# Five experts with a fixed place instead of four, and the first group of four as the fourth unit

## The chip, the core and the metric

The kernel runs on one core of a Trainium2 chip. The time is the device time of one execution in microseconds. Three runs of the kernel before gave 1578.7, 1586.66 and 1594.92 us; the median is 1586.66 us.

## What is computed

A decoder trunk of two layers over 272 tokens (16 meta tokens and 256 of x) of width 1024. Each layer is a mixer, a layer norm, a mixture of experts and a layer norm again. The mixers differ and are not touched here. The mixture is the same in both layers:

```
scores = sigmoid(h @ w_router)                       # 64 experts
idx    = the 8 best of the 4 best groups of 8, by scores + bias
w      = 2.5 * scores[idx] / sum(scores[idx])
out    = sum over idx of w * (silu(h @ w_gate[e]) * (h @ w_up[e])) @ w_down[e]
out   += (silu(h @ sh_gate) * (h @ sh_up)) @ sh_down   # one shared expert
```

All weights are float32. An expert has 1024 x 512 gate and up weights (2.097 MB, "gate_up") and 256 x 1024 down weights (1.049 MB), 3.146 MB in all. Every layer reads all 64 experts. The last layer needs only the 256 tokens of x.

## The kernel before

**Units.** The 64 experts are sorted by how many tokens chose them and worked through in 27 units (`WIDTHS`, L67). A unit is a pair (64 rows for each of two experts) or a group of four (32 rows each), so that every unit fills TensorE's 128 rows. The ranks 0 to 43, the fullest experts, go into the pairs, the ranks 44 to 63 into the groups. Before, the units are two pairs, then four times a group and four pairs, then four pairs and a last group: the groups are units 2, 7, 12, 17 and 26. The experts are counted in the order of the units as j = 0 to 63; `rank_at(j)` gives the rank that sits at place j. If an expert had more tokens than its rows, a further round over all pairs would follow (`more_rounds`).

**Fixed experts.** Loading has to start before the routing is known. `FIXED` experts (0 to 3) get the first ranks whatever their tokens are: their sort key has 1e5 added (in `constants`). Their weights are loaded during the mixer before (`load_first_experts`, and by hand in layer 0). The expert at place 4 of the kernel before has rank 44, which is known only when the sort is done.

**Slots.** The weights live in `RING` = 6 slots. Slots 0 to 3 are plain buffers ("upper" in layer 0, "experts" in layer 1). Slot 4 lies in `dense_ring`, half 0, where the shared expert's gate and up weights are until they are used. Slot 5 has its gate_up in "upper" (layer 0) or `x_gate_up` (layer 1) and its down weights in `dense_ring`. `assign_slots` (L86) says which slot each place j gets: the places that are loaded when unit i is done are `LOADS[i]`, and they take the slots which the unit frees, in the order of `FREED_ORDER` where that names the unit.

**One unit on TensorE** (L1795 on): gate_up (L1832), the turn of the next unit's rows (L1811), the turn of the product (L1867), the combination of the unit before into the sum (L1852 in layer 0, L1850 in layer 1), the spread of places for a unit three ahead (L1385, L1386), and down (L1887). Behind unit 2 stand the missing halves of the shared expert (L1348), in unit 3 its down product (L1903).

**The load queue** is SP's, one queue in program order. For unit i (`experts_after`) it waits until gate_up of the unit is done (in the first units for its first half, then the second), issues the gate_up loads into the freed slots, waits until down is done and issues the down loads. Behind unit 2 it waits for the shared halves and issues the gate_up of the expert in the shared slot; its down weights are issued in unit 3, after the shared down product.

**Around the routing** (`norm_and_route`): TensorE turns the scores (L1518), VectorE picks the experts, ScalarE copies the turned rows of the tokens, GpSimd stores them to DRAM (L1495) and gathers the rows of units 0 and 1 (L1420). VectorE sorts the experts (`order`, L1684). SP loads the shared down weights (L1247), waits for the order, and loads the expert at place 4 into slot 5. A barrier ends the block, and the first turn of gathered rows follows (L1811). In layer 0 the region of slot 5's gate_up first holds the router's scaled weights and the scores; they are read for the last time when the scores are turned.

## Time and profile before

| | |
|---|---|
| median of three runs | 1586.66 us |
| the profiled execution | 1585.79 us |
| its span | 1583.9 us |
| TensorE busy | 1451.9 us, 92% |
| VectorE busy | 687.2 us, 43% |
| load queue (q1) | 481.81 MB, 76.9% of 16 engines' span |
| gathers and stores from GpSimd (q0) | 29.05 MB |
| experts of layer 0 | unit 0 from 438.11 us, last group from 898.53 us |
| experts of layer 1 | unit 0 from 1092.14 us, last group from 1551.90 us |

TensorE's busy time includes what the profile models of its ends, so 92% is not 92% of its peak. The page divides the span into 40 slices; in the two expert stages (slices 13 to 23 and 29 to 39) DMA stands at 9 tenths or more with 413 to 425 GB/s, and TensorE mostly at 9, with a 7 where it waits. The shares over the whole span therefore mean little: a change of the experts has to be read from what ends last in those two stages.

### The profile page before, as it was taken

To read this page: it belongs to the slowest core of one execution; us is meant where nothing else is said; L and a number is where in the kernel's file an instruction comes from. 1 tells how busy PE (TensorE), PEld (TensorE's weight loads), DVE (VectorE), ACT (ScalarE), POOL (GpSimd) and SP (SyncE) were. 2 spreads that over 40 slices of the span, in tenths; PEclk is the share of its full clock that TensorE was granted. 3 is DMA by queue.
4 is the path that set the end of the run, shared out by engine and by line. 5 is a ranking of instruction groups with operands and counts; after the bars stand their busy time and mean duration, and the time that the engine had idled before them with its cause. 6 is when DMAs were issued, how large, how long until landed. Compare 5 with 4: busy or idle time off the path is not lost. (4 is left out here: it accounts for less than half of the span.)

```text
span 1583.9 us, 24378 instructions
## 1 busy us (share of the span) xinstructions
PE 1451.9 (92%) x9414; PEld 858.7 (54%) x9414; DVE 687.2 (43%) x1459; ACT 355.3 (22%) x744; POOL 251.2 (16%) x323
## 2 busy tenths in 40 slices
PE   8999888999799999797999979897999999979996
PEld 6788668887546444343454457773443433424442
DVE  3888738731524343333343349034333332323324
ACT  3766455220410111111111130123101111101111
POOL 5789606200100000000000000001000000000000
PEclk9999999899899999898999988998999999989998
DMA  7669362039399999999999973297999999999994
GB/s 275 213 187 241 118 181 80 2 114 394 106 379 422 422 423 425 421 424 423 419 425 421 413 272 149 66 403 288 417 425 421 423 422 424 423 424 421 425 421 190
DMA packets 105968, 512.44 MB, mean 324 GB/s; under 512 B 37220, under 2 KB 42404, under 8 KB 68732
## 3 DMA queue, kind: packets, MB, share of 16 engines
q1 hardware_dynamic: 96028, 481.81, 76.9%
q0 software_dynamic: 9824, 29.05, 4.9%
q8 instruction: 77, 1.26, 0.3%
q14 instruction: 39, 0.32, 0.1%
HBM read 508.92 MB, written 17.10 MB: 332 GB/s over the span
## 5 line engine op out<-in xcount | busy, mean ns | idle before, releaser
L2041 DVE TENSOR_TENSOR e_ac<-e_sl,banks 128x256 f32<-128x256 f32 x54 | 22.7, 421 | 408.1 <-ACT e_sl L1959 408.1
L1832 PE MATMUL banks<-upper,e_xgT 128*64 128x512 f32 (+1 forms) x880 | 195.9, 612 | 2.3 <-DMA upper<-in_moe_gate_up 2.1
L327 PE MATMUL banks<-hT,dense_ring 128*128 128x272 f32 x768 | 185.5, 400 | 5.1 <-DMA dense_ring<-in_w_in 5.1
L1420 POOL DMA_INDIRECT x_xg<-rows_dram,x_idx x54 | 53.8, 996 | 829.7 <-DVE x_idx L1412 823.6
L327 PEld LDWEIGHTS banks<-hT,dense_ring 128*128 128x128 f32 x768 | 147.3, 193 | 39.9 <-DMA dense_ring<-in_w_in 5.4
L1832 PE MATMUL banks<-dense_ring,e_xgT 128*64 128x512 f32 (+1 forms) x288 | 136.2, 629 | 35.7 <-issue 35.7
L1832 PE MATMUL banks<-experts,e_xgT 128*64 128x512 f32 (+1 forms) x720 | 160.8, 609 | 1.3 <-DMA experts<-in_moe_gate_up 1.1
L1959 ACT ACTIVATE e_sl<-banks 128x256 f32<-128x256 f32 x54 | 20.8, 385 | 496.1 <-PE banks L1832 496.1
L1832 PEld LDWEIGHTS banks<-upper,e_xgT 128*64 128x64 f32 (+1 forms) x880 | 64.9, 131 | 90.1 <-issue 90.1
L1852 PE MATMUL banks<-x_sg,route_consts 128*128 128x272 f32 x432 | 104.4, 393 | 0.5 <-DVE acc L2028 0.5
L1850 PE MATMUL banks<-route_consts,x_sg 128*128 128x512 f32 x216 | 97.6, 594 | 0.8 <-DVE acc L2025 0.8
L1832 PEld LDWEIGHTS banks<-dense_ring,e_xgT 128*64 128x64 f32 (+1 forms) x288 | 38.0, 134 | 104.1 <-issue 104.1
L1832 PEld LDWEIGHTS banks<-experts,e_xgT 128*64 128x64 f32 (+1 forms) x720 | 52.9, 132 | 75.9 <-issue 75.9
L2055 DVE COPY route_consts<-banks 128x512 f32<-128x512 f32 x54 | 37.4, 692 | 127.3 <-PE banks L1887 125.3
L2008 DVE TENSOR_TENSOR acc<-acc,banks 128x272 f32<-128x272 f32 x208 | 89.8, 438 | 6.1 <-PE banks L1852 3.0
L1852 PEld LDWEIGHTS banks<-x_sg,route_consts 128*128 128x128 f32 x432 | 79.9, 190 | 17.4 <-issue 1.7
L1887 PE MATMUL banks<-experts,e_aT 128*64 128x512 f32 (+1 forms) x360 | 80.2, 596 | 5.1 <-DVE acc L2013 4.8
L1887 PE MATMUL banks<-dense_ring,e_aT 128*64 128x512 f32 (+1 forms) x304 | 80.0, 595 | 3.6 <-DVE acc L2013 3.0
L1887 PE MATMUL banks<-upper,e_aT 128*64 128x512 f32 (+1 forms) x360 | 80.2, 596 | 1.2 <-DVE acc L2008 1.2
L2013 DVE TENSOR_TENSOR acc<-acc,banks 128x512 f32<-128x512 f32 x100 | 68.8, 688 | 22.3 <-PE banks L1850 19.8
L497 DVE SCALAR_TENSOR_TENSOR upper<-route_consts,conv_w,upper 128x272 f32<-128x272 f32 x64 | 54.1, 845 | 49.4 <-ACT upper L385 38.3
L1832 PE MATMUL banks<-x_gate_up,e_xgT 128*64 128x512 f32 (+1 forms) x160 | 75.0, 624 | 0.0
(453 smaller groups left out, 2130.2 us busy)
## 6 DMA issues: line engine op xcount, KB each, us to landing
upper<-in_moe_gate_up SPq DMA_DIRECT2D x45, 2048.0 KB, 28.0
experts<-in_moe_gate_up SPq DMA_DIRECT2D x36, 2048.0 KB, 27.7
upper<-in_moe_down SPq DMA_DIRECT2D x43, 1024.0 KB, 26.5
experts<-in_moe_down SPq DMA_DIRECT2D x43, 1024.0 KB, 26.5
dense_ring<-in_moe_down SPq DMA_DIRECT2D x38, 1024.0 KB, 25.7
dense_ring<-in_moe_gate_up SPq DMA_DIRECT2D x18, 2048.0 KB, 20.5
dense_ring<-in_w_in SPq DMA_DIRECT2D x47, 512.0 KB, 5.1
upper<-in_moe_gate_up SPq DMA_DIRECT2D x20, 1024.0 KB, 13.3
```

Source lines behind the costliest of these rows:

```text
L327: mm = pe.matmul(ps[g % 4][:, 0:T], slot[:, n % SLOTS_IN, c, :], hT[:, c, :], start=(c == 0), stop=(c == DC - 1))
L497: step.done(dve.scalar_tensor_tensor(out=dst, in0=src[:, j:j + T], scalar=w(j), in1=dst, op0=ALU.mult, op1=ALU.add))
L1420: pool.indirect_dma_start(out=ex["xg"][:, i % 2, :], out_offset=None, in_=mem["rows_dram"], in_offset=bass.IndirectOffsetOnAxis(ap=ex["idx ...
L1832: mm = pe.matmul(gub[e * n:(e + 1) * n, :], xgT[:, i % 2, c, e * n:(e + 1) * n], gate_up_weights(mem, j)[:, c, :], start=(c == 0), stop=(c ...
L1850: pe.matmul(cb[m][:], sg[:, i % 4, tokens], ys[:, columns], start=True, stop=True).then_inc(cmm, 1)
L1852: pe.matmul(cb[m % 4][:, 0:W], ys[:, m * P:(m + 1) * P], sg[:, i % 4, :], start=True, stop=True).then_inc(cmm, 1)
L1887: mm = pe.matmul(yb[e * n:(e + 1) * n, :], aT[:, f, e * n:(e + 1) * n], down_weights(mem, j)[:, f, h * BLOCK:(h + 1) * BLOCK], start=(f == ...
L1959: act.activation(sl[:], gub[:, 0:FF], ACT.Silu).then_inc(sil, 1)
L2008: dve.tensor_tensor(acc[:, m, 0:W], acc[:, m, 0:W], cb[m % 4][:, 0:W], ALU.add).then_inc(addd, 1)
L2013: dve.tensor_tensor(total[:, tile, columns], total[:, tile, columns], cb[m][:], ALU.add).then_inc(addd, 1)
L2041: dve.tensor_tensor(ac[:], sl[:], gub[:, FF:], ALU.mult).then_inc(mul, 1)
L2055: dve.tensor_copy(ys[:, BLOCK:], y1b[:]).then_inc(ye1, 1)
```

## The change

Five experts (0 to 4) have a fixed place. The widths start with three pairs and end with three pairs and a group, so the groups are units 3, 8, 13, 18 and 26. Place 4 is now rank 4, in the third pair; its weights go to slot 5 as before, but SP no longer waits for the order: in layer 0 it waits until the scores are turned, in layer 1 for nothing. `HELD` = 4 keeps what `FIXED` meant for the loads that are issued before the routing. The shared expert still goes with units 2 and 3; the expert that takes its slot is place 11 (before 13). With `FREED_ORDER` down to one entry, the groups of the new kernel sit in slots 1, 2, 3 and 0, and the slots 5 and 4 always hold pairs.

```diff
-FIXED = 4
+FIXED, HELD = 5, 4
...
-WIDTHS = (2, 2) + 4 * (4, 2, 2, 2, 2) + (2, 2, 2, 2, 4)
+WIDTHS = (2, 2, 2) + 4 * (4, 2, 2, 2, 2) + (2, 2, 2, 4)
...
-FREED_ORDER = {2: (0, 5, 1, 2, SHARED_SLOT), 7: (SHARED_SLOT, 5, 1, 2)}
+FREED_ORDER = {2: (0, RING - 1, SHARED_SLOT)}
...
-                for j in range(FIXED):
+                for j in range(HELD):
                     load_down(sp, k, mem, 0, j, j)
...
-def load_expert(sp, k, mem, layer, j):
-
-    load_gate_up(sp, k, mem, layer, expert_at(sp, mem, j), j)
-    load_down(sp, k, mem, layer, expert_at(sp, mem, j), j)
-
-
-def load_first_experts(sp, k, mem, layer, js=range(FIXED)):
+def load_first_experts(sp, k, mem, layer, js=range(HELD)):
...
                 load_shared_down(sp, k, mem, layer)
-                sp.wait_ge(ordered, 1)
-                load_expert(sp, k, mem, layer, FIXED)
+                if layer == 0:
+                    sp.wait_ge(score_turned, 1)
+                load_gate_up(sp, k, mem, layer, HELD, HELD)
+                load_down(sp, k, mem, layer, HELD, HELD)
...
-                dve.tensor_copy(mem["order"][:], sort_ps[0:1, 0:E]).then_inc(ordered, 1)
+                dve.tensor_copy(mem["order"][:], sort_ps[0:1, 0:E])
...
-            "down_low_ready": [sem(f"down_low_{slot}_ready") for slot in range(FIXED)],
+            "down_low_ready": [sem(f"down_low_{slot}_ready") for slot in range(HELD)],
```

The slots of the first places, as the tables give them (place: slot; in brackets the places that are loaded when the unit is done):

```
before                                        after
unit 0  0:0 1:1            (5 6)              unit 0  0:0 1:1            (5 6)
unit 1  2:2 3:3            (7 8)              unit 1  2:2 3:3            (7 8)
unit 2  4:5 5:0 6:1 7:2    (9 10 11 12, 13)   unit 2  4:5 5:0            (9 10, 11)
unit 3  8:3 9:0            (14 15)            unit 3  6:1 7:2 8:3 9:0    (12 13 14 15)
unit 4  10:5 11:1          (16 17)            unit 4  10:5 11:4          (16 17)
```

The number behind a comma is the expert in the shared slot.

SP in the block of layer 0's routing, before. `in_sh_down` are the shared down weights, `order` the sorted experts, `in_moe_gate_up` and `in_moe_down` the weights of the expert at place 4:

```order
L1247 DMA dense_ring<-in_sh_down 128x2x1024
L1257 TENSOR_LOAD order
L1257 ISA x2
L1202 ISA
L1202 DMA upper<-in_moe_gate_up 128x4096
L1257 TENSOR_LOAD order
L1257 ISA x2
L1221 ISA
L1221 DMA dense_ring<-in_moe_down 128x2048
L1477 UNCONDITIONAL_BRANCH
```

The same place after the change:

```order
L1247 DMA dense_ring<-in_sh_down 128x2x1024
L1202 DMA upper<-in_moe_gate_up 128x4096
L1221 DMA dense_ring<-in_moe_down 128x2048
L1471 UNCONDITIONAL_BRANCH
L1743 UNCONDITIONAL_BRANCH
```

The two loads follow the shared down weights with no value read from `order` between them.

TensorE in layer 0 from the end of unit 2's down product to unit 3, before. 32x512 is a product of a group, 64x512 one of a pair; L1348 are the shared expert's halves:

```order
L1887 MATMUL banks<-dense_ring,e_aT 32x512
L1887 MATMUL banks<-upper,e_aT 32x512 x3
L1348 MATMUL banks<-hT,dense_ring 128x272 x16
L1832 MATMUL banks<-upper,e_xgT 64x512 x16
L1811 MATMUL banks<-ident,x_xg 128x128 x8
L1867 MATMUL banks<-ident,e_ac 128x128 x2
L1903 MATMUL banks<-shared_act,dense_ring 128x272 x16
```

And after the change:

```order
L1883 MATMUL banks<-dense_ring,e_aT 64x512
L1883 MATMUL banks<-upper,e_aT 64x512
L1342 MATMUL banks<-hT,dense_ring 128x272 x16
L1828 MATMUL banks<-upper,e_xgT 32x512 x32
L1807 MATMUL banks<-ident,x_xg 128x128 x8
L1863 MATMUL banks<-ident,e_ac 128x128 x2
L1899 MATMUL banks<-shared_act,dense_ring 128x272 x16
```

The pair now stands before the shared halves and the group behind them.

## Rows read from the trace of the kernel before

**Rows 1.** A stretch: busy PE, PEld, DVE, ACT, POOL; clock, DMA share, GB/s.

```profile
740.00:760.00 20.00, 10.24 (x67) 3.04 (x68) 0.00 (x0) 0.25 (x1) 0.00 (x0) 0.66 1.00 419
```

**Rows 2.** Timeline of TensorE, layer 0: start, duration, line, form, idle before and releaser.

```profile
467.72 7.07 PE L1832 MATMUL banks<-upper,e_xgT 128*32 128x512 f32 x64
...
492.52 7.09 PE L1832 MATMUL banks<-upper,e_xgT 128*64 128x512 f32 x32
...
655.60 1.03 PE L1832 MATMUL banks<-dense_ring,e_xgT 128*32 128x512 f32 x1 [8.79 <-issue]
...
749.76 1.03 PE L1832 MATMUL banks<-dense_ring,e_xgT 128*32 128x512 f32 x1 [10.74 <-issue]
...
898.53 3.64 PE L1832 MATMUL banks<-upper,e_xgT 128*32 128x512 f32 x32
...
904.29 3.64 PE L1832 MATMUL banks<-upper,e_xgT 128*32 128x512 f32 x32 [2.12 <-DMA upper<-in_moe_gate_up]
```

**Rows 3.** Timeline of SP's load queue, layer 0.

```profile
430.31 0.38 SPq L1202 DMA_DIRECT2D upper<-in_moe_gate_up  x1
...
441.95 4.27 SPq L1209 DMA_DIRECT2D upper<-in_moe_gate_up  x4
...
471.66 5.21 SPq L1209 DMA_DIRECT2D upper<-in_moe_gate_up  x8
...
493.33 0.33 SPq L1202 DMA_DIRECT2D dense_ring<-in_moe_gate_up  x1
499.80 0.85 SPq L1202 DMA_DIRECT2D upper<-in_moe_gate_up  x2
```

**Rows 4.** Timeline, all engines, of layer 0's routing.

```profile
408.54 0.39 PE L1518 MATMUL banks<-ident,upper 64*128 64x64 f32 x3 [0.86 <-ACT upper L1580]
...
418.80 0.58 POOL L1495 DMA_DIRECT2D rows_dram<-acc  x1 [18.72 <-ACT acc L1591]
```

**Rows 5.** A stretch of 2 us before the first reload of layer 0.

```profile
440.00:442.00 2.00, 2.00 (x13) 0.72 (x10) 0.00 (x0) 0.00 (x0) 0.99 (x1) 1.00 0.02 6
```

**Rows 6.** Timeline of SP's load queue, layer 1.

```profile
1062.96 5.75 SPq L1247 DMA_DIRECT2D dense_ring<-in_sh_down  x1
...
1088.01 0.01 SPq L1221 DMA_DIRECT2D dense_ring<-in_moe_down  x1
1096.64 4.27 SPq L1209 DMA_DIRECT2D experts<-in_moe_gate_up  x4
...
1156.57 0.86 SPq L1202 DMA_DIRECT2D experts<-in_moe_gate_up  x2
```

**Rows 7.** A stretch of 2 us behind the shared expert's loads, layer 1.

```profile
1074.00:1076.00 2.00, 0.00 (x0) 0.00 (x0) 1.76 (x9) 2.00 (x5) 0.00 (x0) 0.50 0.49 199
```

**Rows 8.** Queue's packets, MB, share: 441.95-499.80; 520-840; 430.31-432.31; 442-444; 1096.64-1156.57; 1080-1084.

```profile
q1 hardware_dynamic: 3003, 21.94, 91.6%
...
q1 hardware_dynamic: 11870, 128.83, 95.7%
...
q1 hardware_dynamic: 17, 0.28, 71.2%
...
q1 hardware_dynamic: 6, 0.05, 7.3%
...
q1 hardware_dynamic: 3148, 22.94, 93.1%
...
q0 software_dynamic: 288, 1.05, 66.0%
```

**Rows 9.** Gathers, issue to landing (last number): at 1085, and the median of all.

```profile
x_xg<-rows_dram,x_idx POOLq DMA_INDIRECT x1, 3.8
...
x_xg<-rows_dram,x_idx POOLq DMA_INDIRECT x54, 10.1
```

**Rows 10.** Timeline of TensorE, layer 1.

```profile
1089.56 1.49 PE L1811 MATMUL banks<-ident,x_xg 128*128 128x128 f32 x8 [2.26 <-PEq L174]
...
1556.62 3.64 PE L1832 MATMUL banks<-experts,e_xgT 128*32 128x512 f32 x32 [1.08 <-DMA experts<-in_moe_gate_up]
```

More of the change, by code:

```diff
@@ L1473, in norm_and_route @@
             "keys_ready", "keys_spread", "ranks_ready", "sorted", "count_ready"))
-        warmed, ordered = sem("table_held"), sem("order_ready")
+        warmed = sem("table_held")
         gain = lambda c: ln[:, 4 * layer * DC + c:4 * layer * DC + c + 1]
```

## The prediction

> **What bounds the kernel.** I read the two expert stages first by 20 us stretches, then the order of TensorE's units, then the load queue (SP). In [rows 1] TensorE is busy 10.24 of 20 us while the 16 DMA engines stay at share 1.00 and 419 GB/s: they have no room left. How close the two are is in [rows 2]: a group of four takes TensorE 7.07 us for its gate and up weights, a pair 7.09 us, so a unit costs the same whatever its width, and twice per layer (at the groups in units 12 and 17) TensorE stands for 8.79 and 10.74 us until the last of four experts lands. The last unit, again a group, starts at 898.53 and stops in its middle until 904.29, where the row names a DMA as releaser; in layer 1 it is the same at 1556.62 [rows 10]. So **each expert stage ends by the DMA engines**: by when they begin to run without a break, by the bytes, and by every break in between. From the two stalls I get the price of one expert, gathers beside it included: (749.76 - 655.60) / 12 = 7.85 us.
>
> **Part 1: expert 4 is loaded early.** Before, its load is issued at 430.31, when the order of the experts is known; the first reload (experts 5 and 6 into the slots that unit 0 frees) goes out at 441.95 [rows 3]. Between 440 and 442 the engines move 6 GB/s [rows 5]: the expert is already in, nobody waits for it. After the change it is loaded in idle time before that (layer 0 when the scores are turned, from 408.54 on [rows 4]; layer 1 straight behind the shared expert). The time of the first reload hangs on unit 0's matmuls, and the number of experts loaded after it is 59 in both kernels. So this part **gains nothing** on the path; its cover is the idle time itself.
>
> It has one cost, in layer 1. The shared expert's last load is issued at 1062.96 [rows 6], and the queue has run out between 1074 and 1076, where 199 of some 422 GB/s leave about 0.9 us of work, so at about 1075 [rows 7]. Expert 4 is 3.15 MB, 7.5 us at 422 GB/s: it ends at 1082.4. The rows of the tokens are stored just then, 1.05 MB between 1080 and 1084 on the other queue [rows 8]; alone they need 2.5 us and are over at about 1082.7. At 1080.1 some 1.0 MB of the expert is left; both together, 2.05 MB, need 4.9 us, so the stores end between 1082.7 and 1085.0. The two gathers wait for them: 3.8 us from issue to landing [rows 9], and TensorE turns the gathered rows at 1089.56 [rows 10]. Nearly all of a delay arrives there. Bounds: nothing lost and 0.7 us gained (SP's last load of expert 4, at 1088.01 [rows 6], no longer stands before the barrier that lets TensorE go at 1089.56), or 2.3 us lost. I take 1.2 us, nearer to the loss, because the overlap of the two transfers is sure and the gain is one of several things the barrier may wait for. In layer 0 the stores start at 418.80 [rows 4] and expert 4 is in by 418: nothing.
> The Trainium skill, "DMA: Bandwidth & Descriptors", section "Queues, rings and completion order", says that an engine takes turns between the queues that have work; by it the stores run at half rate while both have bytes and all of the 2.3 us is lost, my upper end. The sum with it would be 1.1 us more.
>
> **Part 2: the pair comes third, the group fourth.** On TensorE the two units only change places, and by [rows 2] every unit starts when it did: unit 2 at 467.72, the halves of the shared expert behind it, unit 3 at 492.52, its gate_up done at 499.6. What changes is how many slots are free. Unit 2 before frees four slots, after it two. SP's queue before: four experts from 471.66 on, the shared slot's expert at 493.33, two more at 499.80 [rows 3]; the engines never pause. After: two experts at 471.66, the shared slot's gate_up at 493.33 (its down weights wait behind, until the shared expert's down product is done), and then nothing until unit 3's gate_up frees four slots at 499.80. So by 499.80 the engines can have moved **at most** experts 5 to 10 and one gate_up: 6 x 3.146 + 2.097 = 20.97 MB. Before, the load queue had moved 21.94 MB by then, and it moves 128.83 MB in 320 us while full, 403 GB/s beside the gathers [rows 8]. The deficit is 0.97 MB = 2.4 us. On top comes the restart: of the load issued at 430.31 only 0.28 MB had moved by 432.31, 0.7 us worth, so it starts 1.3 us after its issue [rows 8]. Issued with a gather under way (441.95), only 0.05 MB had moved by 444, so up to 2.0 us. I take 1.3, since no gather is due at 499.80. **Layer 0: 2.4 + 1.3 = 3.7 us.** Does the earlier hole (experts 9 and 10 landed, 493.33 not yet reached) add to it? No: the gate_up issued there needs 1.3 + 5.2 us and is in at 499.8, so the cap of 20.97 MB is just reached. With a restart of 2.0 us it is missed by 0.7: 5.1 us is the upper end, 2.4 the lower.
> Layer 1, the same way: first reload at 1096.64, unit 3's loads at 1156.57 [rows 6]; 22.94 MB moved in between [rows 8]. Deficit 1.97 MB = 4.9 us, with the restart **6.2 us**, between 4.9 and 7.6.
>
> **Where it goes.** From 500 on the queue is never empty again: four experts at 499.80, as in the groups later. The lost time is not made up, because the engines are the bound at the end of both layers: the waits before 904.29 and 1556.62 mean that a later last expert is later one for one. TensorE's own chain shifts with it (the last group starts 9 units after the group in unit 17 before, 8 units after the one in unit 18 now; (898.53 - 749.76) / 9 = 16.5 us less, against two experts more, 15.7 us), so it stays just behind the engines. All other edits (the removed semaphore, the load that takes a constant instead of a value from the order, the names) cost nothing: DVE and SP have no one behind them there.
>
> **Sum:** 3.7 + 6.2 + 1.2 = 11.1 us on the profiled execution's 1585.79, so 1596.9; the median of the runs shown is 1586.66, 0.9 above. I forecast **1597 us**, 0.7% slower. The ends of the unknowns give 2.4 + 4.9 - 0.7 = 6.6 and 5.1 + 7.6 + 2.3 = 15.0 us.
>
> **Rivals.**
> The forecast (the engines run dry once in each layer, around unit 3): chance 0.62.
> *No hole, or one that is hidden*: the times of SP's issues or the last unit move so that the 2.12 and 1.08 us waits of TensorE swallow it. For it: only 1 to 2 MB are missing. Against: the waits are TensorE's for the engines, not the reverse. 1.2 us remain: 1588. Chance 0.18.
> *Faster*: the load of expert 4 between 430 and 440 did hold up what follows, and with it gone each layer ends one expert, 7.85 us, sooner: 1586.66 - 15.7 = 1571. It decides if the first reload after the change goes out, or lands, several microseconds sooner. Against it stands the empty stretch of [rows 5]. The Trainium skill, "Trainium Kernel Development and Optimization", section "Best Practices", asks to overlap transfers with compute, which is what this load does; by that rule alone the load's move is a gain. Chance 0.06.
> *Slower by more than 1%*: the routing of layer 1 pays. A gather issued while the load queue is full lands after 10.1 us, the median of all 54, against 3.8 us for the one at 1085 [rows 9]. If stores and gather meet expert 4's stream at that price, unit 0 starts 6.3 us late, and the sum is 3.7 + 6.2 + 6.3 = 16.2: 1603. It decides if the stream is still running when the gather is issued. Against it: the stream should be over at 1082.4. Chance 0.13.
> *The order of the experts overflows*: with five fixed experts the first expert in a group of 32 rows could have more than 32 tokens, and a whole extra round of 32 pairs would follow, 64 x 7.85 = 502 us. Counted with the reference on its inputs, that expert has 30 tokens in layer 0 and 29 in layer 1, before and after. Chance 0.01.
>
> **Range and chances.** Runs of the kernel before spread from 1578.7 to 1594.92, so about 1% (16 us) is what tells a change from none. The range reaches from the hidden case less 3 us to the 15.0 us end and the rival behind it, with 3 us for the runs' own spread: 1585 to 1606. Faster by over 1%: the third case, 0.06. Slower by over 1% (1602.5): 0.08 of the fourth case, the fifth, and 0.08 of the forecast's own: 0.17. Between: 0.77.
>
> **What the profile after would show.** The load of expert 4 at about 409 and 1069; the same start of unit 0 in layer 0 and up to 2 us later in layer 1; unit 3 as the first group at 492 with DMA below full share between about 492 and 501, and again around 1148 to 1158; the groups in units 13 and 18 standing for about 11 us each; the last wait still on a DMA, at about 908 and 1568. If the engines are full through 490 to 502, part 2 is wrong; if the stretch is empty and the end has not moved, the claim on the bound is; if the first reload is not at 442, part 1 is.

## The result and the profile after

The kernel after takes 1597.68 us, the median of 11 runs; ten of them lie between 1588.39 and 1600.19 us. The kernel before takes 1587.34 us in 11 runs (1578.7 to 1594.92). The ratio is 1.0046 with a 95% interval of 1.0026 to 1.0065: 7 us slower, between 4 and 10, well under 1%. (One of the 11 runs of the kernel after, 8270.28 us, was disturbed; it is left out of the ratio, and without it the median is 1596.58 us, 9.2 above before.) The forecast was 1597 us.

The profiled execution of the kernel after is its fastest, 1588.39 us, and a reader who compares it with the 1585.79 us of before sees 2.6 us where the medians show 10. So the traces have to be compared by stretches. Unit 0 of layer 0 starts at 430.60 instead of 438.11, by stretches whose work the change does not touch: 5.4 us are the luck of one execution, 2.1 us are TensorE's clock in layer 0's routing (again_after, below). Behind it the stages take longer than they did.

First the order of TensorE's units in layer 0, as in [rows 2]: start, duration, line, form, idle time before and releaser. 128*32 is a product of a group, 128*64 one of a pair.

```profile
460.08 2.34 PE L1828 MATMUL banks<-upper,e_xgT 128*64 128x512 f32 x10
...
484.84 1.50 PE L1828 MATMUL banks<-upper,e_xgT 128*32 128x512 f32 x12
...
667.64 1.94 PE L1828 MATMUL banks<-upper,e_xgT 128*32 128x512 f32 x8 [11.81 <-issue]
...
761.80 2.79 PE L1828 MATMUL banks<-upper,e_xgT 128*32 128x512 f32 x12 [10.98 <-issue]
...
894.65 3.64 PE L1828 MATMUL banks<-upper,e_xgT 128*32 128x512 f32 x32 [0.43 <-issue]
...
899.48 1.06 PE L1828 MATMUL banks<-upper,e_xgT 128*32 128x512 f32 x8 [1.19 <-DMA upper<-in_moe_gate_up]
```

Unit 2 starts 29.5 us behind unit 0, as before (467.72 - 438.11 = 29.6), and unit 3 24.8 us later, as before, now as a group. The groups in units 13 and 18 stand for 11.8 and 11.0 us, and the last wait of the last group is still one for a DMA. From unit 0 to the end of that wait it is 899.48 - 430.60 = 468.88 us against 904.29 - 438.11 = 466.18: **2.7 us more**.

Next the load queue, as in [rows 3]:

```profile
403.59 0.34 SPq L1202 DMA_DIRECT2D upper<-in_moe_gate_up  x1
...
434.46 4.44 SPq L1209 DMA_DIRECT2D upper<-in_moe_gate_up  x4
...
463.89 5.28 SPq L1209 DMA_DIRECT2D upper<-in_moe_gate_up  x4
476.63 0.33 SPq L1221 DMA_DIRECT2D upper<-in_moe_down  x1
477.14 0.33 SPq L1221 DMA_DIRECT2D dense_ring<-in_moe_down  x1
485.66 0.34 SPq L1202 DMA_DIRECT2D dense_ring<-in_moe_gate_up  x1
492.12 1.98 SPq L1202 DMA_DIRECT2D upper<-in_moe_gate_up  x4
```

Expert 4 goes out at 403.59; the first reload comes 3.86 us behind unit 0's start (before: 3.84), so the early load has not brought it forward. Behind unit 2 stand two experts (four halves at 463.89 where [rows 3] show eight), the shared slot's gate_up, and nothing more until 492.12. What the engines did meanwhile stands in two stretches of layer 0 and five of layer 1 (busy PE, PEld, DVE, ACT, POOL; clock, DMA share, GB/s):

```profile
484.00:486.00 2.00, 2.00 (x16) 0.82 (x19) 0.44 (x1) 0.00 (x0) 0.00 (x0) 1.00 0.60 250
...
492.00:494.00 2.00, 2.00 (x14) 1.71 (x14) 1.31 (x3) 1.22 (x3) 0.00 (x0) 1.00 0.82 213
...
1144.00:1146.00 2.00, 2.00 (x11) 1.77 (x10) 0.00 (x0) 0.00 (x0) 0.00 (x0) 1.00 0.26 107
1146.00:1148.00 2.00, 2.00 (x20) 0.74 (x22) 0.42 (x1) 0.00 (x0) 0.00 (x0) 1.00 0.00 0
1148.00:1150.00 2.00, 2.00 (x24) 0.54 (x20) 0.00 (x0) 0.00 (x0) 0.00 (x0) 1.00 0.85 197
...
1154.00:1156.00 2.00, 2.00 (x12) 1.29 (x11) 1.30 (x3) 0.96 (x3) 0.00 (x0) 1.00 0.76 164
1156.00:1158.00 2.00, 2.00 (x6) 0.86 (x5) 0.69 (x1) 0.00 (x0) 0.00 (x0) 1.00 0.86 360
```

Each layer has two breaks: one when the six experts are in (484, 1144), and one when the shared slot's gate_up is all but in too (492, 1154). In layer 1 the engines move nothing at all for over 2 us. TensorE is busy throughout: its row shows nothing of the loss.

In layer 1, as in [rows 10]:

```profile
1086.95 1.09 PE L1807 MATMUL banks<-ident,x_xg 128*128 128x128 f32 x8 [2.18 <-DMA x_xg<-rows_dram,x_idx]
...
1089.13 3.46 PE L1828 MATMUL banks<-experts,e_xgT 128*64 128x512 f32 x10
...
1559.34 1.92 PE L1828 MATMUL banks<-experts,e_xgT 128*32 128x512 f32 x16 [1.18 <-DMA experts<-in_moe_gate_up]
```

Unit 0 to the last wait: 1559.34 - 1089.13 = 470.21 us, before 1556.62 - 1092.14 = 464.48: **5.7 us more**. The routing of layer 1, from its first column sum to unit 0's gate_up, took 31.62 us (from 1060.52) and takes 33.60 us (from 1055.53): **2.0 us more**. The stretch between the layers (156.23 and 156.05 us) and the tail (27.28 and 27.26 us) are as they were. That makes 2.7 + 5.7 + 2.0 = 10.4 us more. Layer 0's routing takes 2.1 us less (37.34 and 39.47 us up to unit 0), which leaves 8.3. The median of the ten undisturbed runs lies 9.2 us above before, the ratio says 7 (4 to 10). That the first sum meets the 10.3 us between the medians of 11 runs is chance.

The stretches of all kernels that were run, each from its one profiled execution, in us; each ratio is to the kernel before in the same set of runs, and again_before is a single run. "Chain" is layer 1's routing up to the issue of the rows' stores (L1491 in the kernel after), "rows" from there to unit 0's gate_up:

| kernel | stage 0 | chain | rows | stage 1 | ratio to before |
|---|---|---|---|---|---|
| before | 466.18 | 18.48 | 13.14 | 464.48 | |
| again_before | 465.99 | 20.18 | 19.65 | 465.57 | |
| after | 468.88 | 18.54 | 15.06 | 470.21 | 1.0046 (1.0026 to 1.0065) |
| again_after | 468.84 | 18.50 | 15.31 | 470.54 | 1.0064 (1.0042 to 1.0086) |
| load_early | 466.49 | 18.48 | 15.84 | 465.01 | 0.9994 (0.9975 to 1.0012) |
| group_fourth_late_load | 469.05 | 18.49 | 12.55 | 470.27 | 1.0059 (1.004 to 1.0078) |
| group_fifth | 475.15 | 21.35 | 12.39 | 476.48 | 1.0112 (1.0081 to 1.0143) |
| shared_short | 467.70 | 20.20 | 13.90 | 464.32 | 0.999 (0.9973 to 1.0007) |
| down_late | 469.01 | 18.49 | 15.35 | 470.62 | 1.0052 (1.003 to 1.0074) |
| shared_behind | 466.34 | 18.50 | 14.71 | 466.21 | 1.0002 (0.9982 to 1.0022) |
| load_at_barrier | 469.45 | 21.41 | 12.42 | 466.71 | 1.0004 (0.9984 to 1.0023) |
| mend_both | 466.35 | 18.49 | 12.08 | 466.77 | 1.0006 (0.9985 to 1.0026) |
| load_when_stored | 469.03 | 20.22 | 19.43 | 470.61 | 1.0077 (1.0052 to 1.0102) |

### The profile page after: what moved, and what is told of

It is laid out like the page before. It is cut to its first block and busy times, and to the rows that moved or that the text cites. A ratio compares the mean times of both kernels' runs of the same rounds, so it can differ in the third digit from the quotient of the medians.

```text
span 1586.6 us, 24344 instructions
## 1 busy us (share of the span) xinstructions
PE 1447.3 (91%) x9414; PEld 855.1 (54%) x9414; DVE 688.1 (43%) x1459; ACT 355.4 (22%) x744; POOL 251.1 (16%) x323
## 5 line engine op out<-in xcount | busy, mean ns | idle before, releaser
L1828 PE MATMUL banks<-experts,e_xgT 128*64 128x512 f32 (+1 forms) x720 | 132.9, 623 | 22.8 <-issue 21.6
L1828 PE MATMUL banks<-dense_ring,e_xgT 128*64 128x512 f32 x288 | 126.9, 594 | 0.0
L1828 PEld LDWEIGHTS banks<-experts,e_xgT 128*64 128x64 f32 (+1 forms) x720 | 45.9, 130 | 101.8 <-issue 101.8
L1883 PE MATMUL banks<-dense_ring,e_aT 128*64 128x512 f32 x304 | 73.0, 597 | 3.6 <-DVE acc L2009 3.0
L1807 PEld LDWEIGHTS banks<-ident,x_xg 128*128 128x128 f32 x432 | 46.2, 141 | 46.9 <-issue 44.3
L1828 PE MATMUL banks<-x_gate_up,e_xgT 128*64 128x512 f32 x160 | 70.5, 593 | 0.0
L1883 PE MATMUL banks<-experts,e_aT 128*64 128x512 f32 (+1 forms) x360 | 65.7, 596 | 5.1 <-DVE acc L2009 4.6
L1883 PE MATMUL banks<-upper,e_aT 128*64 128x512 f32 (+1 forms) x360 | 65.7, 596 | 1.6 <-DVE acc L2004 1.2
```

The lines of the kernel that those rows point to most:

```text
L1807: mm = pe.transpose((t0b, t1b)[c // 4][:, (c % 4) * P:(c % 4 + 1) * P], xg[:, i % 2, c * P:(c + 1) * P], ident[:])
L1828: mm = pe.matmul(gub[e * n:(e + 1) * n, :], xgT[:, i % 2, c, e * n:(e + 1) * n], gate_up_weights(mem, j)[:, c, :], start=(c == 0), stop=(c ...
L1883: mm = pe.matmul(yb[e * n:(e + 1) * n, :], aT[:, f, e * n:(e + 1) * n], down_weights(mem, j)[:, f, h * BLOCK:(h + 1) * BLOCK], start=(f == ...
```

## The experiments

### The two kernels once more

again_after is the kernel after, unchanged.

> The kernel after once more, for how far the stretches of one kernel differ from one execution to another. Theory: layer 0's expert stage 468.9 us and layer 1's 470.2 us within 0.5, layer 1's routing 33.6 us within 0.8; the start of unit 0 in layer 0 at about 438 us, as in the five other executions, and not at the 430.6 of the profile of the kernel after, where the stretches that the change does not touch happened to be shorter by 7.5 us. Rival: the early load shortens the way to unit 0 in layer 0, and it starts at 431 again.

1597.94 us (10 runs). The expert stages repeat to 0.04 and 0.33 us. Layer 0's routing starts at 398.18 (after: 393.26, before: 398.64), so the two profiles of one kernel differ by 4.9 us ahead of it; unit 0 starts at 435.51. Another 2.1 us, between the start of routing and unit 0, appears in both profiles of this kernel (37.34 and 37.33 us against 39.47) and in none of the others, though seven of those load expert 4 at the same point of layer 0 (39.0 to 39.6 us). It is therefore not the early load. The traces show it as TensorE's clock. Eight products of the shared expert (L1342) make 1.6 of the 2.1 us: they take 2.10 us at a granted clock of 1.00 in the kernel after (418.6 to 420.6 us) and 3.70 us at 0.50 in the kernel before (L1348, 424.6 to 426.6). The other 0.5 goes with the second turn of the tokens' rows ahead of them, 1.87 against 2.82 us. Why the clock rises earlier in these two is not shown.

again_before is the kernel before, unchanged.

> The kernel before once more: one look. Expert stages 466.2 and 464.5 us within 0.5, routing of layer 1 31.6 us within 0.8, unit 0 of layer 0 at about 438 us.

Stage 0 repeats to 0.2 us (465.99), stage 1 only to 1.1 (465.57, 0.6 outside what was expected). The routing of layer 1 does not repeat: 39.83 us instead of 31.62, 1.7 of the difference in the chain and 6.5 behind the stores. The timeline of GpSimd and SP shows why; here in the kernel before

```profile
1085.25 1.06 POOL L1420 DMA_INDIRECT x_xg<-rows_dram,x_idx  x1 [4.81 <-DVE x_idx L1412]
...
1086.53 0.30 SPq L1202 DMA_DIRECT2D x_gate_up<-in_moe_gate_up  x1
```

and in again_before, with TensorE's first turn of the gathered rows:

```profile
1088.91 1.06 POOL L1420 DMA_INDIRECT x_xg<-rows_dram,x_idx  x1 [5.57 <-DVE x_idx L1412]
...
1089.70 0.36 SPq L1202 DMA_DIRECT2D x_gate_up<-in_moe_gate_up  x1
...
1098.52 1.97 PE L1811 MATMUL banks<-ident,x_xg 128*128 128x128 f32 x8 [7.99 <-DMA x_xg<-rows_dram,x_idx]
```

Where the fifth expert's load comes 1.28 us behind the gather, the rows are turned 4.3 us after the gather's issue; where it comes 0.79 us behind, after 9.6 us, and TensorE stands for 8 us. The trace of again_before shows how. Between 1090.9 and 1096.9 us the load queue completes 127 packets with 2.01 MB and the gather's queue 117 with 0.24 MB: the two go on nearly packet for packet, but a packet of the gather carries an eighth of the bytes. In the kernel before the gather's queue had completed 134 packets between 1086.5 and 1088.5, beside 13 of the load. The prediction did not know this second case of the kernel before, since the one trace at hand had the first.

### Each part alone

load_early: the order of the units as before, the early load as after. The expert at place 4, rank 44, is computed with expert 4's weights.

```diff
-                sp.wait_ge(ordered, 1)
-                load_expert(sp, k, mem, layer, FIXED)
+                if layer == 0:
+                    sp.wait_ge(score_turned, 1)
+                load_gate_up(sp, k, mem, layer, FIXED, FIXED)
+                load_down(sp, k, mem, layer, FIXED, FIXED)
```

> The kernel before with part 1 alone: the load of the fifth place is issued when it is in the kernel after (behind the scores' turn in layer 0, straight behind the shared expert in layer 1) and brings expert 4's weights; the order of the units, slots and reloads stays that of before. The expert that has rank 44 is then computed with expert 4's weights. Theory (the place of the group costs 2.7 and 5.7 us, the early load costs only the routing of layer 1): layer 0 from unit 0's gate_up to the last group's wait 466.2 us (465.7 to 466.7, as before), layer 1's routing 33.6 us (2.0 more than the 31.6 before), layer 1's expert stage 464.5 us as before; whole kernel 1.5 to 2.5 us above before, ratio about 1.0013. Rival A (the early load also costs the expert stages, since the queue is empty when the first reload comes): the stages are 1 to 3 us longer than before. Rival B (the late load held up the first reload): the stages are up to 7.85 us shorter each.

1588.19 us (12 runs). Stages 466.49 and 465.01 us: neither rival. The routing of layer 1 takes 34.32 us, 2.7 more than in the profile before. The median does not show it: 1.0 us less than before, between 4 less and 2 more, where 1.5 to 2.5 more were expected. The two traces of the kernel before suggest why: it is spared these 2 to 3 us, but in one of the two its late load cost 6.5 us between stores and unit 0 (19.65 against 13.14). How often that happens was not counted, so this is not shown.

group_fourth_late_load: the order of the units as after, the load as before.

```diff
-                if layer == 0:
-                    sp.wait_ge(score_turned, 1)
+                sp.wait_ge(ordered, 1)
                 load_gate_up(sp, k, mem, layer, HELD, HELD)
```

> The kernel after with part 1 taken back: the load of expert 4 waits for the order of the experts again, as before; the group stays the fourth unit. Theory: layer 1's routing is back at 31.6 us (31.2 to 32.0), the expert stages keep the loss of the kernel after (468.9 in layer 0, 470.2 in layer 1, each within 0.7); whole kernel 8 to 9 us above before, ratio about 1.0053. Rival (the delay of the routing in layer 1 is not from the two transfers that meet, but from run to run): routing stays at 33 to 34 us. Rival (the loss needs both parts together): the stages return to 466.2 and 464.5.

1598.85 us (9 runs), 9.4 us above before (6.3 to 12.4). Stages 469.05 and 470.27, routing 31.04. The parts add up in the traces: the stages' loss belongs to the order of units alone, the routing's to the early load alone.

### More and less of the same

group_fifth delays the first group by one more pair.

```diff
-WIDTHS = (2, 2, 2) + 4 * (4, 2, 2, 2, 2) + (2, 2, 2, 4)
+WIDTHS = (2, 2, 2, 2) + 4 * (4, 2, 2, 2, 2) + (2, 2, 4)
```

> The kernel after with a fourth pair ahead of the first group of four, which is then the fifth unit; later groups are one unit later too, and one pair less stands ahead of the last group. Theory (until the first group's gate_up, only the two slots that each pair frees, and the shared one, can be filled): nine experts, 28.3 MB, can be moved by the end of the first group's gate_up at 516.3, which takes some 71 us at 403 GB/s from 435.8 on, so the engines stand for about 10 us in layer 0 and 12 us in layer 1. Against 2.7 and 5.7 us for the fourth unit, layer 0's expert stage is then 475 to 478 us and layer 1's 475 to 478 us, the kernel 16 to 22 us above before, ratio about 1.012. Rival (a fixed cost of moving the units, such as another order of gathers and matmuls): both stages stay within 1 us of the kernel after (468.9, 470.2). Rival (the wait just moves to the later groups): TensorE's waits ahead of the groups shrink and the stages' ends stay.

1609.08 us (4 runs), 1.0112. The stages take 475.15 and 476.48 us, 9.0 and 12.0 more than before. With the group third, fourth and fifth, layer 0's stage is 466.2, 468.9 and 475.2 us, layer 1's 464.5, 470.2 and 476.5. The breaks are longer, here ahead of the group's gate_up and at its end:

```profile
492.00:496.00 4.00, 4.00 (x20) 1.37 (x22) 0.44 (x1) 0.00 (x0) 0.00 (x0) 1.00 0.68 209
...
512.00:516.00 4.00, 4.00 (x21) 1.56 (x20) 1.67 (x6) 0.97 (x2) 0.71 (x1) 1.00 0.34 143
516.00:520.00 4.00, 4.00 (x38) 1.20 (x40) 0.69 (x1) 0.00 (x0) 0.27 (x1) 1.00 0.75 267
```

shared_short keeps the group fourth and lets TensorE reach it sooner; 7/8 of the shared expert's gate_up products behind unit 2 are left out.

```diff
-                       start=(c == 0), stop=(c == DC - 1))
+                       start=(c == 0 or len(cs) == 1), stop=(c == DC - 1))
...
-                            shared_half(pe, mem, ex, hN, sh_ps[j], j)
+                            shared_half(pe, mem, ex, hN, sh_ps[j], j, range(DC - 1, DC))
```

> The kernel after with the shared expert's gate_up products behind unit 2 cut to one of their eight chunks (7/8 of that part of the computation is left out). TensorE then reaches the group in unit 3 some 6.6 us sooner in layer 0 and 9.2 us sooner in layer 1, and its gate_up ends before the six experts and the shared slot's gate_up can have been loaded. Theory (the engines run dry because the group frees its slots too late): the queue is never empty, and the loss is gone: layer 0's expert stage 466.2 us (465.5 to 467), layer 1's 464.5 us (463.8 to 465.5), although TensorE is given 6.6 and 9.2 us. Rival (TensorE bounds the stages): they get shorter by all of 6.6 and 9.2 us, to 462 and 461. Rival (the loss comes from another place, such as the restart of the queue alone or the order of the gathers): they stay at 468.9 and 470.2.

1588.68 us (10 runs). The stages take 467.70 and 464.32 us. TensorE reached the group 6.4 us sooner behind unit 0 in layer 0 and 9.0 us sooner in layer 1 (1144.06 - 1095.63 = 48.4 against 1146.58 - 1089.13 = 57.5 us). The median is 9.0 us below that of the kernel after, which ran in another set; the two stages together gained 7.1: layer 1's gained 5.9, which is the break, and not 9.0. Layer 0's gained 1.2 of the 2.7 us, 0.7 short of the range expected, although the engines now have work where the break was (486 to 506 us shows 401 to 446 GB/s throughout):

```profile
492.00:494.00 2.00, 2.00 (x18) 1.09 (x11) 0.55 (x2) 0.52 (x2) 0.00 (x0) 1.00 1.05 446
```

In the first 57.7 us behind the first reload the load queue moved 21.86 MB, as in the kernel before (21.87). So the break is mended in layer 0 too, and 1.5 us above before remain that come later. Why is open (see "Layer 0, 3.7 us" below).

### The loss mended with nothing left out

shared_behind puts the shared expert's missing halves behind the group's gate_up instead of ahead of it.

```diff
@@ TensorE
                     gate_up(i)
+                    for j in range(ahead, 2 * FC) if i == SHARED_UNIT + 1 else ():
+                        if j == FC:
+                            pe.wait_ge(ye0, i)
+                            pe.wait_ge(ye1, i)
+                        shared_half(pe, mem, ex, hN, sh_ps[j], j)
                     if i + 1 < N:
                         turn(i + 1)
...
                     down(i)
-                    if i == SHARED_UNIT:
-                        for j in range(ahead, 2 * FC):
-                            if j == FC:
-                                pe.wait_ge(ye0, i + 1)
-                                pe.wait_ge(ye1, i + 1)
-                            shared_half(pe, mem, ex, hN, sh_ps[j], j)
@@ SP, behind unit 3's gate_up
-                        for e, j in zip(es, js):
+                        for n, (e, j) in enumerate(zip(es, js)):
+                            if i == SHARED_UNIT + 1 and n == 2:
+                                sp.wait_ge(ex["sh_gu"], 2 * FC)
+                                load_gate_up(sp, k, mem, layer, expert_at(sp, mem, SHARED_NEXT), SHARED_NEXT)
                             load_gate_up(sp, k, mem, layer, e, j)
```

> The kernel after, with nothing left out: the rest of the shared expert's gate_up products (16 matmuls in layer 0, 24 in layer 1) moves from behind unit 2 to behind the gate_up of unit 3, the group, so that the group frees its slots 7.5 and 10.5 us sooner; SP loads two gate_ups of the freed slots, then the one of the shared slot, then the other two. Theory (the engines wait for the group's slots): the six experts are in just when the group's gate_up ends, the queue is never empty, layer 0's expert stage is 466.2 to 467.7 us and layer 1's 464.3 to 465.5 us (2 and 5.5 us less than in the kernel after), the whole kernel 5 to 8 us below the kernel after and 0 to 3 above the kernel before. Rival (TensorE pays: the activations of unit 3 come later by the shared products): a new stall in units 3 and 4, but the stages gain as far as the DMA engines end them, so this shows in the waits ahead of the groups in units 8 and 13 only; if it decides, the stages stay at 468.9 and 470.2.

1589.87 us (12 runs), ratio 1.0002 (0.9982 to 1.0022): 8.1 us less than the kernel after beside it (1597.94). Stage 0 takes 466.34 us, what it took before; stage 1 takes 466.21, 4.0 less than after, but 1.7 more than before and 0.7 more than expected. TensorE and SP in layer 0, and the stretch of layer 1 in which the six experts are in:

```profile
484.04 7.08 PE L1828 MATMUL banks<-upper,e_xgT 128*32 128x512 f32 x64
491.05 7.60 PE L1342 MATMUL banks<-hT,dense_ring 128*128 128x272 f32 x32
...
491.33 0.85 SPq L1202 DMA_DIRECT2D upper<-in_moe_gate_up  x2
499.39 0.33 SPq L1202 DMA_DIRECT2D dense_ring<-in_moe_gate_up  x1
...
1150.00:1152.00 2.00, 2.00 (x11) 1.77 (x10) 0.00 (x0) 0.00 (x0) 0.00 (x0) 1.00 0.79 270
```

The group's slots are free 8.4 us sooner (the first load into them 491.33 - 438.25 = 53.1 us behind unit 0, in the kernel after 492.12 - 430.60 = 61.5), just when the queue would run out: the same TensorE work in another order, and in layer 0 the break is all but gone. In layer 1 two short ones are left, 270 GB/s at 1150 and 229 GB/s from 1160 to 1162, together about 1.6 us at 420 GB/s, which is the size of the 1.7 us that stage 1 still lacks. The second has a plain cause: two gate_ups, 4.2 MB or 10.4 us at 403 GB/s, are issued at 1148.80, and the next one, for the shared slot, only at 1159.89, because it waits for the shared expert's products, which now stand behind the group's gate_up. The rival (later activations of unit 3) does not decide in layer 0; in layer 1 nothing shows that it costs more than these breaks.

### The price in the routing of layer 1

down_late holds only expert 4's down weights back in layer 1.

```diff
                 load_gate_up(sp, k, mem, layer, HELD, HELD)
+                if layer > 0:
+                    sp.wait_ge(stored, 16 * sum(len(token_tiles(la)) for la in range(layer + 1)))
                 load_down(sp, k, mem, layer, HELD, HELD)
```

> The kernel after, but in layer 1 the down weights of expert 4 (1.05 MB) are loaded only when the rows are stored; its gate_up weights (2.1 MB) stay where they are. Theory (the stores wait for the stream of expert 4): its gate_up weights are in before the rows are stored, stores to gathers takes 5.5 to 6.3 us as in the kernels with the late load instead of 8.8, and the routing of layer 1 takes 31.0 to 32.5 us instead of 33.6 to 34.3; 1 to 2.5 us less in all. Rival (the gathers then meet the down weights and lose as much): stores to gathers is short again, but the rows land late and the routing stays at 33.5 to 34.5 us. Expert stages as in the kernel after.

1597.85 us (12 runs). The rival was right: from the stores' issue to the gather's it is 6.75 us instead of 8.79, but the rows are turned 5.55 us after the gather instead of 4.09, because the down weights go out at 1089.01, ahead of the gather at 1089.88. Routing 33.84 us: nothing gained.

load_when_stored holds all of expert 4 back to that point.

```diff
                 if layer == 0:
                     sp.wait_ge(score_turned, 1)
+                else:
+                    sp.wait_ge(stored, 16 * sum(len(token_tiles(la)) for la in range(layer + 1)))
                 load_gate_up(sp, k, mem, layer, HELD, HELD)
```

> The kernel after, but in layer 1 expert 4's whole load waits for the rows to be stored, which is what the first gather waits for too, so the load is issued with or ahead of the gather. Theory (a load issued within a microsecond of the gather buries it): stores to gather is short again (5.5 to 7 us), the rows land 9 to 10.5 us after the gather's issue, and the routing of layer 1 takes 38 to 41 us: 5 to 7 us more than in the kernel after. Rival (the two queues share fairly and 3.15 MB cost the gather no more than 1 to 2 us): rows after 5 to 6 us, routing 33 to 35 us.

1601.64 us (9 runs), 1.0077. The load goes out at 1090.61 and 1090.99, the gather at 1091.49, and TensorE stands for the rows:

```profile
1100.95 1.97 PE L1809 MATMUL banks<-ident,x_xg 128*128 128x128 f32 x8 [7.74 <-DMA x_xg<-rows_dram,x_idx]
```

9.46 us after the gather. That is again_before's long case made on purpose. The routing takes 39.65 us, 6.1 us more than in the kernel after: 1.7 of them are a longer chain (20.22 and 18.54), 4.4 lie between the stores and unit 0 (19.43 and 15.06).

load_at_barrier starts from the kernel before and moves its late load, in both layers, from the wait for the order to the start of the expert stage.

```diff
@@ routing
-                sp.wait_ge(ordered, 1)
-                load_expert(sp, k, mem, layer, FIXED)
@@ expert stage, SP
+                load_expert(sp, k, mem, layer, FIXED)
                 for i in range(N):
                     if LOADS[i]:
                         experts_after(i)
```

> The kernel before, with nothing left out and only this changed: the load of the fifth place does not wait for the order on the load queue in the routing, but is the first thing that queue does in the expert stage, in both layers. In one of the two executions of the kernel before, this load was issued 0.79 us behind layer 1's first gather (1089.70 and 1088.91), and the rows landed 9.6 us after the gather's issue, with routing 39.8 us; in the other it came 1.28 us behind it, rows after 4.3 us, routing 31.6 us. Theory (a load that comes within a microsecond of the gather buries it): the load is now issued 2 us or more behind the gather, the routing of layer 1 is 31.0 to 32.0 us in this execution, expert stages 466.2 and 464.5 us within 0.8, and the median is 0 to 4 us below the kernel before, as often as that meets the long case. Rival (the load is needed that early): unit 2's or unit 0's chain waits for the fifth expert and the stages grow by 1 to 3 us. Rival (the 39.8 us come from elsewhere, such as TensorE's clock): the median does not move.

1589.75 us (12 runs), ratio 1.0004. The load is issued 5.05 us behind layer 1's gather (1098.51 and 1093.46) and the rows come after 4.51 us. The routing took 33.83 us all the same, because in this execution its chain up to the stores took 21.41 us instead of 18.5; from the stores on it is 12.42 us, as short as anywhere. But the rival decides in layer 0: the load goes out at 436.02, 4.96 us ahead of the first reload at 440.98, and stage 0 takes 469.45 us, 3.3 more than before; stage 1 takes 2.2 more. What is loaded so late must be carried before the reloads.

mend_both adds to shared_behind the same move, in layer 1 alone.

```diff
                 if layer == 0:
                     sp.wait_ge(score_turned, 1)
-                load_gate_up(sp, k, mem, layer, HELD, HELD)
-                load_down(sp, k, mem, layer, HELD, HELD)
+                    load_gate_up(sp, k, mem, layer, HELD, HELD)
+                    load_down(sp, k, mem, layer, HELD, HELD)
@@ expert stage, SP
+                if layer > 0:
+                    load_gate_up(sp, k, mem, layer, HELD, HELD)
+                    load_down(sp, k, mem, layer, HELD, HELD)
```

> The kernel shared_behind (the kernel after with the rest of the shared expert's gate_up products behind the group's gate_up) with one more edit: in layer 1 expert 4's load is the first thing that the load queue does in the expert stage; in layer 0 it stays where the kernel after has it. Nothing is left out. Theory (the two costs of the change are the late freeing of the group's slots and the stores that meet expert 4's stream): routing of layer 1 back to 31.0 to 32.0 us, layer 0's expert stage 466.3, layer 1's 465 to 467 us (expert 4's load ends about when the first reload starts); 1.5 to 2.5 us below shared_behind, whole kernel 1585 to 1589 us, level with the kernel before or up to 3 us below it. Rival (expert 4's load runs into the first reload): what the routing gains, layer 1's stage loses.

1588.21 us (12 runs), ratio 1.0006 (0.9985 to 1.0026). Routing 30.57 us, the shortest of all, stage 0 466.35, stage 1 466.77: by the sum of its stretches it is the best version of the changed order with nothing left out, and the span of its profiled execution, 1583.9 us, is that of the kernel before. Against the kernel before it is no gain that can be measured. None of the kernels beats it.

The stores themselves show what expert 4's stream does to them: DMA issues of that moment, with KB each and us to landing, in the kernel before and in the kernel after.

```profile
rows_dram<-acc POOLq DMA_DIRECT2D x2, 512.0 KB, 4.3
```

```profile
rows_dram<-acc POOLq DMA_DIRECT2D x2, 512.0 KB, 6.4
...
x_gate_up<-in_moe_gate_up SPq DMA_DIRECT2D x1, 2048.0 KB, 13.5
dense_ring<-in_moe_down SPq DMA_DIRECT2D x1, 1024.0 KB, 15.7
```

The stores were issued at 1074.07 and 1074.95; expert 4's last weights, issued at 1064.26, landed at 1080.0. With no load beside them the stores land after 3.3 us (mend_both, group_fourth_late_load, load_at_barrier) to 4.7 us (again_before, load_when_stored), with the stream after 5.9 (again_after) to 6.6 us (shared_behind).

## Why the prediction was right, point by point

**The bound.** Right. The stages end at a wait for a DMA in every kernel that was run, and in shared_short TensorE's 9.0 us of layer 1 were worth only the 5.9 of the break.

**Part 1 gains nothing.** Right for the stages: load_early leaves them at 466.49 and 465.01. But the prediction took the old load's place to be harmless, and it is not: issued 0.79 us behind the gather or 0.88 us ahead of it, it costs 6 to 7 us (19.65 and 19.43 us from stores to unit 0 in again_before and load_when_stored, against 13.14 and 12.5). Removing that is a gain of part 1 which the prediction did not have, neither in its sum nor among its rivals; the "faster" rival looked for it in the reloads. It may be why load_early's median shows no loss; that was not counted. The kernel after would have the same gain in it, and still stood 9.9 us above before in the later set of runs (1597.94 and 1588.03).

**Part 1 costs 1.2 us in layer 1.** The mechanism was right, the size too small. The step that failed is the choice within 0 to 2.3 us: the stores landed 2.1 us later (6.4 against 4.3), and unit 0 came 1.9 us later counted from the stores' issue, 2.7 in load_early. Stores without a load beside them vary by 1.4 us from kernel to kernel (3.3 to 4.7), so the size is known to about a microsecond only. The upper end, by which the stores end when all the bytes of both are moved, was the better value. The Trainium skill, "DMA: Bandwidth & Descriptors", section "Queues, rings and completion order", has the engines take turns, packet by packet, between queues that have work. For these stores the trace agrees with the size (2.1 us late, where the upper end was 2.3) and not with the turns: from 1075 to 1077 us in the kernel after the load queue completed 104 packets (0.77 MB) and the stores 11 (0.04 MB), in load_early from 1084 to 1086 it was 103 and 4. The stores ran behind the stream rather than at half rate beside it, and the prediction's upper end is the same by either. For the gather of again_before the turns do show (127 and 117 packets), and because its packets are small they leave it an eighth of the load's bytes. The cost also depends on the chain ahead: in group_fifth the stores came 2.9 us later, the stream was over, and the rows took 12.39 us.

**Layer 0, 3.7 us: measured 2.7.** Of bytes the term was right. Between the first reload and 450 us later the load queue had moved, before and after:

```profile
q1 hardware_dynamic: 17738, 180.62, 95.6%
```

```profile
q1 hardware_dynamic: 17235, 179.05, 95.2%
```

1.57 MB less, 3.9 us at 403 GB/s. In the first 57.7 us it was 21.87 against 20.86 MB, 2.5 us; the rest, 1.4 us, has the size of the restart (213 GB/s from 492 to 494, 328 in the next 2 us). What failed, by 1 us, is what the prediction took for granted, that a later queue ends the stage later one for one: at the end of the last wait 185.47 MB had been moved before and 185.08 MB after. That wait ended with 0.39 MB, 1.0 us, less on the queue. Perhaps less of the loads that stand behind the awaited half had gone beside it; no run shows it. shared_short goes the other way: 0.35 MB less than before after 450 us, and its last wait ended with 0.39 MB more on the queue (185.86), together 1.9 us, which is about the 1.5 us that its stage 0 still lacks. So the byte count at which this stage ends moves by 1 us either way with the order of the units, and the cause stays open.

**Layer 1, 6.2 us: measured 5.7.** The same: 181.17 against 178.66 MB after 450 us, 2.51 MB or 6.2 us, and 185.03 against 184.78 MB at the last wait, 0.6 us back. Some 0.5 us of the stage's 5.7 lie ahead of the first reload, which comes 4.96 us behind unit 0 instead of 4.50 (load_early: 4.85).

**"The earlier hole does not add."** Half right. Both breaks are there, and the one at 484 us exists just as long as the shared slot's gate_up waits for TensorE; the total of bytes came out as computed (20.86 of at most 20.97 MB), because that gate_up was all but in at 492, when unit 3's gate_up ended.

**The slack in front of the stages' end.** That TensorE's own chain stays just behind the engines held: the last group waited 1.19 and 1.18 us instead of 2.12 and 1.08.

**The sum.** Partly luck. The stages were forecast 1.5 us too long and the routing 0.8 us too short, which cancels in part; the clock in layer 0's routing took off 2.1 us that the sum did not have; and the measured ratio is worth 7 us (4 to 10), so the forecast's 11.1 lies just above that interval although its 1597 us lies beside the median.

**Rivals.** A hidden hole (1588), a gain of one expert per layer (1571), a layer 1 routing at the full queue's price (1603) and a further round did not come. The third was near: its price, rows after some 10 us, is real, but it belongs to a load issued with the gather, which is how the kernel before does it.

## What to carry to other kernels

With a ring of slots that the DMA engines must never leave idle, count at each point in time the bytes that the freed slots allow, not the number of slots: a wide unit is a large deposit of free slots, and each narrow unit put ahead of it draws the queue down, by 2.7 to 5.7 us here for the first pair and another 6.3 for the second. The repair that worked here, 8.1 us of the loss, is to run other TensorE work behind the products that free the slots instead of ahead of them. And look at what a large load is issued next to: beside a small transfer that an engine waits for, less than a microsecond in the order of issue decided over 6 us here.

## What the runs showed of the hardware that was not expected

- A gather of 128 rows lands after 3.8 to 4.5 us when a 3.15 MB load is issued 1.1 us or more behind it, and after 9.4 to 9.6 us when the load is issued 0.8 us behind it or 0.9 us ahead of it (again_before, load_when_stored). With 1.05 MB ahead of it it lands after 5.5 us (down_late). Once both are under way, they complete nearly as many packets (127 and 117 in 6 us of again_before), of 16 KB for the load and 2 KB for the gather. Where the load went first (load_when_stored), the gather moved nothing in the first 4 us behind its issue.
- Stores of 1.05 MB that meet a load stream get no such turns: 11 packets against 104 in the 2 us from 1075 in the kernel after; they run when the stream is over.
- The stretches that the DMA engines bound repeat to 0.0 to 0.3 us between the two profiles of the kernel after (468.88 and 468.84; 470.21 and 470.54) and to 0.2 and 1.1 us between those of the kernel before, while the start of layer 0's routing, with the same code, lies anywhere from 393.26 to 399.51 us. A change of a few us is read from stretches, not from one execution's total.
- The chain of layer 1's routing takes 18.5 us in eight of the thirteen profiles and 20.2 to 21.4 us in five. The long ones differ at their start: in the five, TensorE's granted clock is 0.50 from 1.5 to 3 us behind the first column sum, in the eight it is 1.00 there. The two column sums take 4.2 us in the kernel before and 6.6 in load_at_barrier. A clock of 0.50 that lasts longer in the middle of the chain (1068 to 1080 us in the kernel after) leaves it at 18.54 us. Why the clock is low at the start of some is open.
